# First stage by blocks of 128 channels, with later weight loads and table; delta rule with both halves transposed in a row

## The chip, the core and the metric

One core of a Trainium2 chip runs the whole program. Its engines work side by side and are tied by semaphores: TensorE (PE; PEld is its weight load), VectorE (DVE), ScalarE (ACT), GpSimd (POOL) and SyncE (SP), which here only issues DMA transfers. The metric is the device time of one execution in microseconds (us). Everything is float32. One `matmul` of the program appears in the trace as two MATMUL records.

## The reference

Two transformer blocks follow each other on a sequence of 1024 tokens of width 1024. The first block has two layers (neighbourhood attention, then grouped-query attention), the second one layer, whose mixer joins latent attention, a gated delta rule and a pooling mixer. Every layer ends in a mixture of experts. Two places matter here. The start of every layer scales and shifts the tokens by numbers made from a conditioning vector `c`:

```
c_act = silu(c)
mod = c_act @ ada_w[l] + ada_b[l]
h = x * (1.0 + scale) + shift
qkv = h @ w_qkv
```

The delta rule works in chunks of 64 tokens: for each chunk and head it forms the products of keys with keys and of queries with keys, multiplies them by decays, solves a unit lower triangular system, and carries a state from chunk to chunk:

```
a_mat = where(strict, (kb @ k.T) * decay, 0)
sol = triangular_solve(a_mat + eye, [v * beta, kb * exp(gc)])
qk = where(incl, (q @ k.T) * decay, 0)
v_new = u_i - w_i @ state
o_i = q_i @ state + qk_i @ v_new
state = state * gl_i + k_i.T @ v_new
```

## The kernel before

The program is a chain of stages with a barrier of all engines between them. Within a stage every engine has its own instruction stream, written by hand, in the order in which the code issues it; what one engine needs of another is a semaphore wait.

**The stage `front`** (lines 271 to 509) computes the scale and shift of the first layer, moves the tokens by them, and multiplies them with the 1024 x 3072 weight `na_w_qkv`. SP loads, in this order: four pieces of 2 MB with the 2048 columns of `ada_w` that hold shift and scale (L344), the tokens' first half (2 MB, L346, `hT`), the first 512 columns of `na_w_qkv` (2 MB, L340, `wt`), and the tokens' second half (2 MB, L348). PE multiplies each piece with the activated `c` (`partial`, L389: output rows of 32 in four column groups of the array, 512 columns each), ACT copies the sums, PE turns them into columns (`columns`, L396), DVE adds the bias and moves the eight channel blocks of the tokens' first half (L479). Only then can the projection begin. It consists of 48 items of eight matmuls each, 128 x 512 (`item`, L419 and L423), in four PSUM banks: item n may start once item n-4 has been evacuated, by DVE where n is even (L504, L449) and by ACT where it is odd (L463, L453).

Beside the projection the same stage computes all other modulation rows. For that SP streams 64 steps of 1 MB (L331) through a ring of four buffers, and DVE multiplies each with its activated `c` and adds it up (`weigh`, L489 and L492), two steps after each item. After item 4q+1, PE adds up quarter q over the partitions (`add_up`, L405). The bias rows for this are loaded by a DMA that repeats each row 32 times (`brow`, L335), at the first step of a quarter. The weights of the third, fourth and fifth block of columns are loaded before steps 18, 34 and 50, the last after the final step. GpSimd clears, fills and spreads the table of position biases for the next stage (L367 to L373, 25 DMAs) as soon as item 0 is done, and stores the finished rows after that.

**The stage `gdn`** (the delta rule, from line 2424 on) handles the eight token tiles in two halves f of four tiles. For each half, DVE normalises queries and keys (L2590) and makes three scaled copies (L2592, L2594, L2597) and two more (L2602, L2603); PE transposes keys, queries and scaled keys (`turn(f)`, L2849), ACT copies the six banks to SBUF (L2728 to L2730), PE multiplies them (`scores(f)`, L2863), and DVE multiplies the products by the decays (`decayed(f)`, L2610 and L2611). Both halves use PSUM banks 0 to 5 for the transposes and 0 to 3 for the products, so `turn(1)` waits until DVE has read `scores(0)`. Then DVE masks the matrices for level 0 of the solution (`level_input`, L2615), writes the decay of the last row of each chunk (`last_decay`, L2571, needed only after the solution), and goes through six levels of the triangular solution (L2636 to L2644), in which PE (L2874) and DVE alternate. ACT applies Silu to the gate `z` (L2747), and GpSimd multiplies it by the gain (L2816) as soon as that is done. In the last part of the stage ACT copies the pooling mixer's means (L2787) and squares the outputs (L2776).

## Time and profile before

| | us |
|---|---|
| Median of three runs | 3713.72 |
| Range of these runs | 3711.33 to 3714.51 |
| The profiled execution, its own time | 3712.36 |
| The profiled execution, its span | 3710.5 |
| PE busy in it | 3417.3 (92%) |
| DVE busy | 1618.9 (44%) |

The span runs from the first to the last instruction; 1.9 us of the execution's own time lie around it. PE is busy for 92% of the span, so the places where PE waits, or runs at the lower clock, are where time can be found. The stage `front` takes from 0 to about 372 us, and PE computes without a break from 34.3 us on. The stage `gdn` takes from 3010 to 3186 us; PE is busy there for a good part of the time, but waits in many short gaps.

### The profile page before, as it was taken

The numbers are of one execution on the slowest core, as the hardware profiler recorded it, in microseconds if no ns is written. First come the engines' busy times: TensorE is split into PE (matmuls) and PEld (weight loads), VectorE is DVE, ScalarE is ACT, GpSimd is POOL, SyncE is SP. The second block draws the span as 40 slices with busy tenths as digits, with TensorE's granted clock in tenths as the row PEclk, the third lists the DMA queues.
The fourth block names the chain that finished last, engine by engine and source line by source line (L and its number), as shares of the span: only waits on it lengthen the run. The fifth ranks groups of instructions, "written<-read, shape, count | busy, mean of one in ns | idle before, by whom it ended". The sixth has DMA issues, their size and how long they took to land. (4 is left out here: it accounts for less than half of the span.)

```text
span 3710.5 us, 51510 instructions
## 1 busy us (share of the span) xinstructions
PE 3417.3 (92%) x20876; PEld 1742.5 (47%) x20876; DVE 1618.9 (44%) x2553; ACT 815.8 (22%) x1815; POOL 364.4 (10%) x355
## 2 busy tenths in 40 slices
PE   7999999899999899999997999998899978998996
PEld 3444565433333344777754333333555658553332
DVE  3760886510111475777756111113332865462114
ACT  0000660100000122555501000000333551111112
POOL 1000300210000000000001200000000920003110
PEclk9999999999999999999998999999999989999998
DMA  9980211599999621000023999997323301319996
GB/s 383 360 318 0 92 67 71 223 409 426 424 423 422 243 91 52 31 1 1 1 92 160 390 426 425 427 421 305 118 81 108 123 1 61 119 65 361 419 418 265
DMA packets 146837, 818.41 MB, mean 221 GB/s; under 512 B 30019, under 2 KB 35779, under 8 KB 100518
## 3 DMA queue, kind: packets, MB, share of 16 engines
q1 hardware_dynamic: 117622, 737.20, 49.9%
q0 software_dynamic: 25808, 68.88, 4.8%
q10 hardware_dynamic: 3168, 8.96, 0.6%
q8 instruction: 172, 2.82, 0.3%
q14 instruction: 67, 0.55, 0.0%
HBM read 752.52 MB, written 82.55 MB: 225 GB/s over the span
## 5 line engine op out<-in xcount | busy, mean ns | idle before, releaser
L2289 PE MATMUL m_yp<-m_w,m_hidT 128*32 128x512 f32 (+2 forms) x2248 | 381.2, 600 | 12.0 <-issue 6.1
L2266 PE MATMUL m_up<-m_w,m_xT 128*32 128x512 f32 (+2 forms) x1792 | 304.2, 605 | 25.9 <-DMA m_w<-in_moe_w_up 25.9
L2266 PE MATMUL m_gp<-m_w,m_xT 128*32 128x512 f32 (+2 forms) x1792 | 297.4, 594 | 8.4 <-DVE m_xT L1910 4.5
L2047 DVE TENSOR_TENSOR m_hid<-m_sg,m_up 128x512 f32<-128x512 f32 x42 | 28.9, 687 | 572.9 <-PE m_up L2266 572.9
L2042 DVE TENSOR_TENSOR m_yt<-m_yp,keep_flat 128x512 f32<-128x512 f32 x128 | 82.4, 685 | 403.8 <-PE m_yp L2289 394.6
L419 PE MATMUL front_acc<-front_hT,front_wt 128*128 128x512 f32 x512 | 224.5, 599 | 5.8 <-DMA front_wt<-in_na_w_qkv 5.8
L2289 PEld LDWEIGHTS m_yp<-m_w,m_hidT 128*32 128x32 f32 (+2 forms) x2248 | 123.0, 124 | 222.7 <-issue 217.7
L2266 PEld LDWEIGHTS m_up<-m_w,m_xT 128*32 128x32 f32 (+2 forms) x1792 | 104.8, 126 | 219.8 <-issue 219.8
L2347 ACT ACTIVATE m_sg<-m_gp 128x512 f32<-128x512 f32 (+1 forms) x64 | 33.5, 524 | 768.7 <-PE m_gp L2266 549.6
L1202 PE MATMUL n_acc<-n_wt,n_hT 128*128 128x512 f32 (+2 forms) x512 | 192.2, 532 | 2.8 <-DMA n_wt<-in_w_in 2.1
L2266 PEld LDWEIGHTS m_gp<-m_w,m_xT 128*32 128x32 f32 (+2 forms) x1792 | 97.4, 123 | 202.3 <-issue 197.1
L253 ACT ACTIVATE gqa_probs<-gqa_scores,gqa_top 128x1024 f32<-128x1024 f32 x128 | 142.5, 1113 | 161.2 <-DVE gqa_top L222 161.2
L912 PE MATMUL n_acc<-n_wt,n_hT 128*128 128x512 f32 x384 | 170.0, 603 | 0.9 <-DMA n_wt<-in_gqa_w_qkv 0.9
L222 DVE TENSOR_REDUCE gqa_top<-gqa_scores 128x1 f32<-128x1024 f32 x128 | 150.7, 1219 | 42.1 <-PE gqa_scores L174 42.1
L2258 PE MATMUL m_gp<-m_w,m_xT 128*32 128x512 f32 (+2 forms) x912 | 155.9, 594 | 6.0 <-DMA m_w<-in_moe_w_up 3.5
L492 DVE SCALAR_TENSOR_TENSOR keep_flat<-v,front_cact,keep_flat 128x2048 f32<-128x2048 f32 x56 | 131.6, 2350 | 65.5 <-DMA v<-in_ada_w 44.6
L419 PEld LDWEIGHTS front_acc<-front_hT,front_wt 128*128 128x128 f32 x512 | 97.7, 192 | 132.0 <-issue 131.3
L1202 PEld LDWEIGHTS n_acc<-n_wt,n_hT 128*128 128x128 f32 x512 | 98.0, 194 | 85.9 <-issue 78.1
L164 PE MATMUL gqa_turn<-keep_ident,gqa_probs 128*128 128x128 f32 x1024 | 137.0, 277 | 0.2 <-ACT gqa_probsT L249 0.2
L164 PEld LDWEIGHTS gqa_turn<-keep_ident,gqa_probs 128*128 128x128 f32 x1024 | 113.6, 142 | 48.9 <-issue 48.9
L174 PE MATMUL gqa_scores<-k1T,q1T 64*128 64x512 f32 x512 | 130.6, 624 | 4.5 <-ACT gqa_probs L253 2.5
L193 PE MATMUL gqa_out<-gqa_probsT,v 128*64 128x128 f32 x2048 | 125.9, 276 | 0.8 <-ACT gqa_probsT L249 0.8
(502 smaller groups left out, 4984.2 us busy)
## 6 DMA issues: line engine op xcount, KB each, us to landing
m_w<-in_moe_w_gate SPq DMA_DIRECT2D x64, 2048.0 KB, 28.7
m_w<-in_moe_w_up SPq DMA_DIRECT2D x64, 2048.0 KB, 27.8
m_w<-in_moe_w_down SPq DMA_DIRECT2D x64, 2048.0 KB, 29.8
v<-in_ada_w SPq DMA_DIRECT2D x40, 1024.0 KB, 12.6
m_w<-in_moe_w_gate SPq DMA_DIRECT2D x32, 1024.0 KB, 28.2
m_w<-in_moe_w_up SPq DMA_DIRECT2D x32, 1024.0 KB, 29.6
m_w<-in_moe_w_down SPq DMA_DIRECT2D x32, 1024.0 KB, 31.0
v<-in_w_mod SPq DMA_DIRECT2D x24, 1024.0 KB, 11.0
```

What stands on the lines that cost most here:

```text
L164: last = pe.transpose(turn[f % TURN][:, i * P:(i + 1) * P], src, ident[:, :])
L174: last = pe.matmul(scores[h][:, c * 512:(c + 1) * 512], qT[half, j, t * P:(t + 1) * P], kT[half, 2 * j // SHARE, c * 512:(c + 1) * 512], s ...
L193: pe.matmul(out[h * HEAD:(h + 1) * HEAD, 0:P], v[:, k, kv * HEAD:(kv + 1) * HEAD], probsT[:, n % 2, h, k], start=k == 0, stop=k == TILES - 1)
L222: dve.tensor_reduce(top[:, n % 2, h:h + 1], scores[h][:, :], AX.X, ALU.max, negate=True).then_inc(max_ready, 1)
L253: act.activation(probs[:, n % 2, h], scores[h][:, :], ACT.Exp, bias=top[:, n % 2, h:h + 1], accum_out=total[:, n % 2, h:h + 1]).then_inc(p ...
L419: last = pe.matmul(acc[n % 4][:, :], wt[:, c % 2, k, i * P:(i + 1) * P], hT[:, k, half * 512:(half + 1) * 512], start=k == 0, stop=k == KC ...
L492: dve.scalar_tensor_tensor(total[:, q % 2], mw[:, s % RING], by, total[:, q % 2], ALU.mult, ALU.add).then_inc(weighed, 1)
L912: last = pe.matmul(acc[t % 2][:, c], hT[:, t % 2, k], wt[:, k, c * 512:(c + 1) * 512], start=k == 0, stop=k == KC - 1)
L1202: last = pe.matmul(acc[c][:, 0:n1 - n0], hT[:, t % 2, k], wt[:, k, n0:n1], start=k == 0, stop=k == KC - 1)
L2258: last = pe.matmul(gp[j][part, :].rearrange("p (m f) -> p m f", m=2), xT[:, j, k, part], w[:, home:home + 2, k * F:(k + 1) * F], start=k = ...
L2266: last = pe.matmul(acc[part, 0:F], xT[:, j, k, part], w[:, place_of[m_, r][0], k * F:(k + 1) * F], start=k == 0, stop=k == KC - 1)
L2289: last = pe.matmul(yp[e][part, :], hidT[:, k, part], w[:, place_of["d", r][0], k * D + e * 512:k * D + (e + 1) * 512], start=k == 0, stop= ...
```

## The change

**In `front`** the first 34 us are cut into channel blocks. The host lays the first 2048 columns of `ada_w` out anew (`first_mod`): piece k holds, for all inputs, the shift and scale of the 128 channels of block k. SP loads one small table (`first_cols`), then for each of the eight k the piece of the modulation (1 MB), the tokens' block (256 KB) and the weights' block (256 KB), then the tokens' second half as before. PE computes block k's partial sums (eight matmuls of 256 columns, two in a row for each of the four column groups), turns them into two columns, and DVE moves the block. As soon as block k is there, PE adds its contribution to the first four items (`by_channels`), two matmuls before the next `partial` and two behind it. Three matmuls on a tile of ones are put ahead. DVE does the first two `weigh` steps inside its loop over k. Items 4 to 47 stay as they were, but `add_up` of the first three quarters comes after items 7, 10 and 13 instead of 5, 9 and 13; the weights are loaded before steps 26, 42 and 58; the bias rows with the fourth step of a quarter; and GpSimd first stores six rows and only then builds the table.

**In `gdn`** DVE normalises both halves first, PE transposes both halves and then multiplies both, with separate PSUM banks for the halves; the transposed banks are handed to ACT one by one; `last_decay` is split and stands after levels 1 and 2; GpSimd multiplies the gate only when `uw_done[0]` is there, after the solution; and ACT squares the first outputs before it copies the pooling means.

The diff, cut to its core, first `front`:

```diff
-    KC, CW, QW, FIRST, RING = D // P, 512, 2048, 4, 4
+    KC, CW, QW, RING, BANKS, LEAD = D // P, 512, 2048, 4, 4, 2
...
-                    if k == 0:
+                    if k == 3:
...
-                first = quarter_of(0)[0]
-                for m in range(FIRST):
-                    sp.dma_start(first_buffer(m), first[:, 2 * m:2 * m + 2, :]).then_inc(first_in[m], 16)
-                sp.dma_start(sel[:, :], a["mod_sel"]).then_inc(s_in, 16)
-                sp.dma_start(hT[:, :, 0:512], xT[:, :, 0:512]).then_inc(x_in[0], 16)
-                load_weights(0)
-                sp.dma_start(hT[:, :, 512:S], xT[:, :, 512:S]).then_inc(x_in[1], 16)
+                sp.dma_start(first_cols[:, :], a["first_cols"]).then_inc(c_in, 16)
+                for k in range(KC):
+                    sp.dma_start(first_buffer(k), a["first_mod"][:, k]).then_inc(m_in[k], 16)
+                    sp.dma_start(hT[:, k, 0:512], xT[:, k, 0:512]).then_inc(x_in[k], 16)
+                    sp.dma_start(wt[:, 0, k], wv[:, k, 0:CW]).then_inc(w0_in[k], 16)
+                sp.dma_start(hT[:, :, 512:S], xT[:, :, 512:S]).then_inc(x1_in, 16)
                 for s in range(RING):
                     load_step(s)
                 load_weights(1)
                 for s in range(RING, STEPS):
-                    if s in (18, 34, 50):
-                        load_weights(2 + (18, 34, 50).index(s))
+                    if s in (26, 42, 58):
+                        load_weights(2 + (26, 42, 58).index(s))
                     load_step(s)
                 load_weights(5)
...
-                pool.wait_ge(mm_done, 1)
+                def store_row(q):
+                    pool.wait_ge(row_added, q)
+                    pool.dma_start(quarter_of(q)[3], row[0:P:32, q % 2]).then_inc(stored[q % 2], 16)
+
+                for q in range(1, 7):
+                    store_row(q)
                 pool.dma_start(flat_table, zero[:, :]).then_inc(cleared, 16)
...
-                for q in range(1, QUARTERS):
-                    dst = quarter_of(q)[3]
-                    pool.wait_ge(row_added, q)
-                    pool.dma_start(dst, row[0:P:32, q % 2]).then_inc(stored[q % 2], 16)
+                for q in range(7, QUARTERS):
+                    store_row(q)
...
-                def partial(m):
-                    pe.wait_ge(first_in[m], 16)
-                    for n in range(2):
-                        k = 2 * m + n
-                        for g in range(4):
-                            last = pe.matmul(mp[32 * g:32 * g + 32, :], cact[:, 0, k:k + 1].to_broadcast([P, 32]),
-                                             first_buffer(m)[:, n, g * CW:(g + 1) * CW], start=k == 0, stop=k == KC - 1)
+                def partial(k):
+                    pe.wait_ge(m_in[k], 16)
+                    if k >= 2:
+                        pe.wait_ge(part_cp, k - 1)
+                    for c in range(KC):
+                        g = c // 2
+                        last = pe.matmul(mps[k % 2][32 * g:32 * g + 32, 0:2 * P], cact[:, 0, c:c + 1].to_broadcast([P, 32]),
+                                         first_buffer(k)[:, c], start=c % 2 == 0, stop=c % 2 == 1)
                     last.then_inc(part_done, 1)
 
-                def columns():
-                    pe.wait_ge(part_cp, 1)
-                    for i in range(4):
-                        last = pe.matmul(ms[:, 4 * i:4 * i + 4], part[:, i * P:(i + 1) * P], sel[:, :], start=True, stop=True)
+                def columns(k):
+                    pe.wait_ge(part_cp, k + 1)
+                    if k >= 2:
+                        pe.wait_ge(cols_done, k - 1)
+                    for i in range(2):
+                        last = pe.matmul(ms[k % 2][:, i:i + 1], part[:, k % 2, i * P:(i + 1) * P], sel, start=True, stop=True)
                     last.then_inc(sum_done, 1)
...
+                def by_channels(k, items):
...
+                    pe.wait_ge(w0_in[k], 16)
+                    pe.wait_ge(h_ready, k + 1)
+                    for n in items:
+                        last = pe.matmul(acc[n][:, :], wt[:, 0, k, n * P:(n + 1) * P], hT[:, k, 0:512], start=k == 0, stop=k == KC - 1)
+                        if k == KC - 1:
+                            last.then_inc(mm_done, 1)
...
+                pe.wait_ge(ones_set, 1)
+                for _ in range(3):
+                    pe.matmul(acc[0][0:32, :].rearrange("p (m n) -> p m n", n=32), ones[:, :], ones[:, :].unsqueeze(1).to_broadcast([P, 16, 32]),
+                              start=True, stop=True)
                 pe.wait_ge(act_done, 1)
...
+                partial(0)
+                columns(0)
+                partial(1)
+                columns(1)
+                for k in range(KC):
+                    by_channels(k, range(0, 2))
+                    if k + 2 < KC:
+                        partial(k + 2)
+                    by_channels(k, range(2, BANKS))
+                    if k + 2 < KC:
+                        columns(k + 2)
+                after = {max(4 * q + 1, 3 * q + 4): q for q in range(1, QUARTERS)}
+                for n in range(BANKS, ITEMS):
                     item(n)
-                    if n % 4 == 1 and n > 4:
-                        q = n // 4
-                        if q < QUARTERS:
-                            add_up(q)
+                    if n in after:
+                        add_up(after[n])
...
+                def move(k, half):
+                    part_of = hT[:, k, half * 512:(half + 1) * 512]
+                    dve.tensor_scalar(part_of, part_of, col[:, 2 * k + 1:2 * k + 2], col[:, 2 * k:2 * k + 1], ALU.mult, ALU.add).then_inc(h_ready, 1)
+
...
+                for k in range(KC):
+                    pair = slice(2 * k, 2 * k + 2)
+                    dve.wait_ge(sum_done, k + 1)
+                    dve.tensor_tensor(col[:, pair], ms[k % 2][:, 0:2], bcol[:, pair], ALU.add).then_inc(cols_done, 1)
+                    dve.wait_ge(x_in[k], 16)
+                    dve.wait_ge(cols_done, k + 1)
+                    move(k, 0)
+                    if k >= KC - LEAD:
+                        weigh(k - KC + LEAD)
+                dve.wait_ge(x1_in, 16)
+                for k in range(KC):
+                    move(k, 1)
+
...
-                    for s in (2 * n, 2 * n + 1):
+                    for s in (2 * n + LEAD, 2 * n + 1 + LEAD):
...
+        TURN_BANK = {"k": ((0, 3), (6, 7)), "q": ((2, 5), (0, 3)), "kb": ((1, 4), (2, 1))}
+        KQ_BANK = (4, 0)
```

then `gdn` and the host:

```diff
-                scale_keys(0)
+                norm_keys(0)
+                norm_keys(1)
+                scale_values(0)
                 scale_rest(0)
-                scale_keys(1)
+                scale_values(1)
                 decayed(0)
                 scale_rest(1)
...
-                last_decay()
...
+                    if 1 <= lv <= 2:
+                        last_decay(lv - 1)
...
                     for m in range(2):
...
+                out_squares(0)
                 act.wait_ge(pool_in, 16 * 5)
                 copy_means(0)
-                out_squares(0)
...
                 pool.wait_ge(z_ready, 1)
+                pool.wait_ge(uw_done[0], 1)
...
+                    pe.wait_ge(normed, f + 1)
                     if f:
-                        pe.wait_ge(qk_ready, 1)
+                        pe.wait_ge(dec_ready, 4)
...
+                    for kind, src in (("k", qkv[:, :, W:2 * W]), ("q", qkv[:, :, 0:W]), ("kb", kb[:, :, :])):
+                        if kind == "q" and f == 0:
                             pe.wait_ge(dec_ready, 2)
-                        if b == 1:
+                        if kind == "kb":
                             pe.wait_ge(kb_ready, f + 1)
                         for m in range(2):
+                            if f and kind != "k":
+                                pe.wait_ge(turns_copied, {"q": 1, "kb": 3}[kind] + (2 * m if kind == "kb" else m))
                             for i in range(4):
                                 t, g = HALF * f + 2 * m + i // 2, i % 2
-                                last = pe.transpose(ps[:, 3 * m + b, i * P:(i + 1) * P], src[:, t, g * P:(g + 1) * P], ident[:, :])
-                    last.then_inc(turned, 1)
+                                last = pe.transpose(ps[:, TURN_BANK[kind][f][m], i * P:(i + 1) * P], src[:, t, g * P:(g + 1) * P], ident[:, :])
+                            last.then_inc(turned, 1)
...
-                    pe.wait_ge(turns_copied, 6 * (f + 1))
+                    pe.wait_ge(turns_copied, 12 if f else 8)
...
                 turn(0)
+                turn(1)
                 scores(0)
-                turn(1)
                 scores(1)
...
+    first_bias = inputs["ada_b"][0, 0:2 * D].reshape(2, D // P, P).transpose(2, 1, 0).reshape(P, 2 * D // P)
+    every_32nd = (np.arange(P)[:, None] % 32 == 0).astype(np.float32)
+    inputs["first_cols"] = np.concatenate([inputs["c"][0].reshape(P, D // P), inputs["c_2"][0].reshape(P, D // P), first_bias, every_32nd], axis=1)
+    inputs["first_mod"] = inputs["ada_w"][0, :, 0:2 * D].reshape(P, D // P, 2, D // P, P).transpose(0, 3, 1, 2, 4).reshape(P, D // P, D // P, 2 * P)
```

What stands in a row on the engines, at three places. First PE at the start of `front`, before:

```order
L389 MATMUL front_mp<-q0T,front_cact 32x512 x16
L389 MATMUL front_mp<-k0T,front_cact 32x512 x16
L396 MATMUL front_ms<-front_sel,front_part 128x4 x4
L419 MATMUL front_acc<-front_hT,front_wt 128x512 x48
L405 MATMUL front_mp<-keep_flat,front_ones 32x512 x4
```

and now (the pattern of the four rows before the last repeats for every block):

```order
L443 MATMUL front_acc<-front_ones 32x512 x3
L394 MATMUL front_mp<-q0T,front_cact 32x256 x8
L403 MATMUL front_ms<-front_first_cols,front_part 128x1 x2
L394 MATMUL front_mp<-q0T,front_cact 32x256 x8
L403 MATMUL front_ms<-front_first_cols,front_part 128x1 x2
L411 MATMUL front_acc<-front_hT,front_wt 128x512 x2
L394 MATMUL front_mp<-q0T,front_cact 32x256 x8
L411 MATMUL front_acc<-front_hT,front_wt 128x512 x2
L403 MATMUL front_ms<-front_first_cols,front_part 128x1 x2
L411 MATMUL front_acc<-front_hT,front_wt 128x512 x2
```

The 32 matmuls of items 0 to 3, which stood in one row behind all partial sums, are now spread between them.

Second DVE between the first modulation and item 0's evacuation in `front` (`front_hT` is moved in place; `keep_flat<-v` is a `weigh` step; `q0T<-front_acc` is the evacuation of item 0), before:

```order
L469 TENSOR_TENSOR front_col<-front_ms,front_bcol 128x16
L472 TENSOR_SCALAR front_col<-front_col 128x4x2
L479 TENSOR_SCALAR front_hT<-front_hT,front_col 128x512 x16
L504 TENSOR_SCALAR q0T<-front_acc 128x512
L489 TENSOR_SCALAR keep_flat<-v,front_cact 128x2048
```

and now, from block 6 on:

```order
L516 TENSOR_TENSOR front_col<-front_ms,front_first_cols 128x2
L506 TENSOR_SCALAR front_hT<-front_hT,front_col 128x512
L499 TENSOR_SCALAR keep_flat<-v,front_cact 128x2048
L516 TENSOR_TENSOR front_col<-front_ms,front_first_cols 128x2
L506 TENSOR_SCALAR front_hT<-front_hT,front_col 128x512
L502 SCALAR_TENSOR_TENSOR keep_flat<-v,front_cact,keep_flat 128x2048
L506 TENSOR_SCALAR front_hT<-front_hT,front_col 128x512 x8
L535 TENSOR_SCALAR q0T<-front_acc 128x512
```

Two `weigh` steps and the eight moves of the second half now stand ahead of the evacuation of item 0.

Third DVE in `gdn`, from the normalisation to level 0, before:

```order
L2590 TENSOR_TENSOR k<-k,keep_raw 128x4x512
L2592 TENSOR_TENSOR gdn_kb<-k,gdn_beta 128x1024
L2594 TENSOR_TENSOR keep_flat<-k,gdn_beta 128x16x64
L2597 TENSOR_TENSOR keep_flat<-k,gdn_nbe 128x16x64
L2610 TENSOR_TENSOR k<-gdn_ps,gdn_dec 128x1024
L2611 TENSOR_TENSOR gdn_KQ<-gdn_ps,gdn_dec 128x16x64
L2602 TENSOR_TENSOR gdn_qd<-k,gdn_eg 128x1024
L2603 TENSOR_TENSOR gdn_KQ<-k,gdn_kdf 128x16x64
L2610 TENSOR_TENSOR k<-gdn_ps,gdn_dec 128x1024
L2611 TENSOR_TENSOR gdn_KQ<-gdn_ps,gdn_dec 128x16x64
L2615 TENSOR_TENSOR gdn_keys<-k,keep_flat 128x1024 x2
L2571 TENSOR_TENSOR gdn_keys<-keep_flat,gdn_glx 64x8x64 x8
```

(these begin with the second half's normalisation), and now, from the normalisation of both halves:

```order
L2621 TENSOR_TENSOR k<-k,keep_raw 128x4x512
L2623 TENSOR_TENSOR gdn_kb<-k,gdn_beta 128x1024
L2621 TENSOR_TENSOR k<-k,keep_raw 128x4x512
L2623 TENSOR_TENSOR gdn_kb<-k,gdn_beta 128x1024
L2628 TENSOR_TENSOR keep_flat<-k,gdn_beta 128x16x64
L2595 SCALAR_TENSOR_TENSOR gdn_nbe<-gdn_eg,gdn_beta 128x32
L2631 TENSOR_TENSOR keep_flat<-k,gdn_nbe 128x16x64
L2636 TENSOR_TENSOR gdn_qd<-k,gdn_eg 128x1024
L2637 TENSOR_TENSOR gdn_KQ<-k,gdn_kdf 128x16x64
L2628 TENSOR_TENSOR keep_flat<-k,gdn_beta 128x16x64
L2631 TENSOR_TENSOR keep_flat<-k,gdn_nbe 128x16x64
L2644 TENSOR_TENSOR k<-gdn_ps,gdn_dec 128x1024
```

The second normalisation has moved ahead of the scaled copies, and the eight rows of L2571 stand no longer ahead of the levels.

## Rows read from the trace of the kernel before

**Rows 1.** Stretches: busy us (count) per engine from PE to POOL, PEclk, DMA share, GB/s

```profile
0.00:34.30 34.30, 12.64 (x72) 3.08 (x73) 4.08 (x10) 2.10 (x3) 0.97 (x6) 0.83 0.97 377
...
3010.00:3068.10 58.10, 35.85 (x334) 27.04 (x336) 41.15 (x50) 29.61 (x49) 4.51 (x1) 0.71 0.00 1
```

**Rows 2.** Timeline, PE in `front`: start, busy us, line, count, [idle before <-releaser]

```profile
8.84 3.64 PE L389 MATMUL front_mp<-q0T,front_cact 128*32 128x512 f32 x16 [8.84 <-ACT front_cact L458]
13.40 1.92 PE L389 MATMUL front_mp<-q0T,front_cact 128*32 128x512 f32 x16 [0.91 <-DMA q0T<-in_ada_w]
...
27.44 1.03 PE L396 MATMUL front_ms<-front_sel,front_part 128*128 128x4 f32 x8 [0.82 <-ACT front_part L453]
34.30 8.09 PE L419 MATMUL front_acc<-front_hT,front_wt 128*128 128x512 f32 x12 [5.84 <-DMA front_wt<-in_na_w_qkv]
...
59.83 10.46 PE L419 MATMUL front_acc<-front_hT,front_wt 128*128 128x512 f32 x24
```

**Rows 3.** Stretches of `front`, columns as in rows 1

```profile
18.30:23.00 4.70, 2.80 (x16) 0.47 (x16) 0.00 (x0) 0.00 (x0) 0.00 (x0) 0.60 1.00 406
34.30:39.50 5.20, 5.20 (x6) 2.16 (x7) 0.00 (x0) 0.00 (x0) 0.00 (x0) 0.50 1.06 397
...
41.10:47.00 5.90, 5.90 (x16) 2.55 (x15) 5.53 (x10) 0.00 (x0) 0.67 (x1) 1.00 1.02 274
```

**Rows 4.** Timeline, DVE in `front`, columns as in rows 2

```profile
28.99 3.74 DVE L479 TENSOR_SCALAR front_hT<-front_hT,front_col 128x512 f32<-128x512 f32 x8
41.13 1.00 DVE L479 TENSOR_SCALAR front_hT<-front_hT,front_col 128x512 f32<-128x512 f32 x2 [8.39 <-DMA front_hT<-in_x_turned]
...
44.78 0.68 DVE L504 TENSOR_SCALAR q0T<-front_acc 128x512 f32<-128x512 f32 x1
...
49.33 2.35 DVE L492 SCALAR_TENSOR_TENSOR keep_flat<-v,front_cact,keep_flat 128x2048 f32<-128x2048 f32 x1 [2.67 <-DMA v<-in_ada_w]
```

**Rows 5.** Timeline, PE in `gdn` where two kinds of 64*64 matmuls meet

```profile
3138.23 0.33 PE L2918 MATMUL gdn_ps<-gdn_KQ,gdn_early 64*64 64x128 f32 x2
3138.26 0.38 PE L2906 MATMUL gdn_ps<-keep_flat,k 64*64 64x128 f32 x3
```

**Rows 6.** Costliest groups of 2621.4 to 2623.2: 16 matmuls into one column group

```profile
L1219 PE MATMUL n_up<-n_latT,n_ukv 128*64 128x128 f32 x16 | 2.0, 276 | 0.0
```

**Rows 7.** Timeline, DVE in `gdn`

```profile
3028.08 2.29 DVE L2590 TENSOR_TENSOR k<-k,keep_raw 128x2048 f32<-128x2048 f32 x1 [0.35 <-ACT keep_raw L2721]
...
3042.05 1.22 DVE L2610 TENSOR_TENSOR k<-gdn_ps,gdn_dec 128x1024 f32<-128x1024 f32 x1
3043.18 1.21 DVE L2611 TENSOR_TENSOR gdn_KQ<-gdn_ps,gdn_dec 128x1024 f32<-128x1024 f32 x1
...
3056.13 1.23 DVE L2610 TENSOR_TENSOR k<-gdn_ps,gdn_dec 128x1024 f32<-128x1024 f32 x1 [9.48 <-PEq L2867]
...
3062.86 5.24 DVE L2571 TENSOR_TENSOR gdn_keys<-keep_flat,gdn_glx 64x512 f32<-64x512 f32 x8
...
3069.28 1.21 DVE L2638 TENSOR_TENSOR k<-keep_flat,gdn_ps 128x1024 f32<-128x1024 f32 x1
...
3092.22 1.22 DVE L2642 TENSOR_TENSOR k<-k,gdn_ps 128x1024 f32<-128x1024 f32 x1 [4.05 <-PE gdn_ps L2874]
```

**Rows 8.** Stretch of `turn(1)` in `gdn`, columns as in rows 1

```profile
3044.45:3049.83 5.38, 5.38 (x24) 4.97 (x24) 2.21 (x2) 0.00 (x0) 0.00 (x0) 0.50 0.00 0
```

**Rows 9.** Timeline, PE in `gdn`

```profile
3052.96 3.03 PE L2863 MATMUL gdn_ps<-gdn_keys 64*64 64x128 f32 x64 [3.13 <-ACT gdn_keys L2730]
3061.95 6.39 PE L2874 MATMUL gdn_ps<-keep_flat,gdn_keys 64*64 64x64 f32 x128 [5.96 <-DVE gdn_keys L2615]
3071.68 6.62 PE L2874 MATMUL gdn_ps<-k,gdn_keys 64*64 64x64 f32 x128 [3.34 <-DVE gdn_keys L2615]
```

**Rows 10.** One line, L2615 of DVE, 3056 to 3070: min/median/max ns, starts

```profile
L2615 DVE TENSOR_TENSOR gdn_keys<-k,keep_flat x2: 1211/2303/3395, 3058.4 to 3061.7; 128x1024 f32<-128x1024 f32 x2
```

**Rows 11.** Timeline, POOL in `gdn`

```profile
3056.21 4.51 POOL L2816 TENSOR_TENSOR gdn_z<-gdn_z,keep_flat 128x2048 f32<-128x2048 f32 x1 [71.38 <-ACT gdn_z L2747]
```

128 lines of the change are left out of this document (55 added, 73 removed).

## The prediction

> **What bounds the kernel now.** I read the stretches first [rows 1]. In the first 34.3 us the DMA engines are busy for 97% at 377 GB/s while PE works for 12.64 us: the DMA bounds. The timeline of PE [rows 2] shows the waits (8.84, 0.91, 0.82, 5.84 us), and that item 0 begins when `na_w_qkv` is there, at 34.30. From then on PE computes without a break, so a start earlier by x ends the stage earlier by x, as long as nothing else becomes late. In `gdn`, PE is busy in 35.85 of the 58.1 us before the levels, at a mean clock of 0.71, so there I read DVE [rows 7]: it computes nearly all the time, except for 9.48 us before 3056.13, in which `turn(1)`, six ACT copies and `scores(1)` follow each other. In the levels PE leads, and DVE waits 4.05 us for it (before 3092.22).
>
> **Front: the DMA side.** 12 MB must land, in the same order of size as before. The tokens' second half, the last of them, makes DVE start at 41.13 [rows 4]; w0, the one before it, was there at 34.30 [rows 2]. At 377 to 406 GB/s [rows 1, 3], 2 MB take 5.2 to 5.6 us, so the second half should land at about 34.2 + 5.4 = 39.6, one DMA issue earlier than its wait on record would say; 41.1 is the late bound. The blocks come every 1.5 MB, 1,572,864 bytes by 0.377 to 0.406 MB/us: 3.9 to 4.2 us (I take 3.9, since the stretch from 18.3 to 23.0 without the beginning ran at 406). All eight blocks are there by 34.2.
>
> **Front: the PE side.** Per block PE has four matmuls of 512 columns, a `partial` and two `columns`. 24 records take 10.46 us at full clock [rows 2], 0.436 each with the odd `add_up`; I use 0.429 and two records to a matmul: 4 x 0.857 = 3.43. The old `partial` is 16 records of 512 in 1.92 us at full clock and 3.64 at half [rows 2]; the new one has 16 records of 256: 0.88 to 0.96. `columns` had 8 records in 1.03 us, at the half clock to judge by its time; four now: 0.26 to 0.52, I take 0.45 with its start. Two changes of the array's shape cost about 0.2 (an estimate: what is left of 1.92 above 16 x 0.429 / 4 = 1.72). Sum 3.43 + 0.88 + 0.45 + 0.2 = 4.95 us, more than the 3.9 of the DMA, so **PE sets the pace**. The second modulation block is there at about 9.6, with its `partial` and `columns` the loop begins at 11.6 to 12.9 and ends after six full rounds and two short ones: 11.6 + 6 x 4.95 + 2 x 3.43 = 48.2; up to 50.8 if part of it runs at half clock. ACT's copies and DVE's first moves (0.47 each, 3.74 for eight [rows 4]) lie beside it.
>
> **Front: what item 4 waits for.** Item 4 needs the moved second half and item 0's evacuation. DVE's stream now has the two `weigh` steps ahead of both. Step 0 and step 1 are the next 2 MB behind the second half: 39.6 + 2.5 = 42.1 and 44.6; the second costs 2.35 [rows 4] and ends at 47.0. Then eight moves, 3.74: 50.7; evacuation 0.68 [rows 4]: **item 4 starts at 51.8** with 0.4 for semaphores. Before, it stood behind item 3 at 34.30 + 32 matmuls: six records took 5.20 us at the half clock [rows 3], the other 58 take 24.9: 64.4. Gain 12.6. But PE then sits idle for 51.8 - 48.2 = 3.6 us. Before 18.3 it idled 3 us and the next stretch ran at 0.60, and after 5.84 us idle at 0.50 for 5.20 us [rows 3], where six records cost 2.6 more than at full clock. I charge 2.2: **net gain of the front 10.4**. With no clock loss and the loop from 11.6 it would be 12.6; with the late bounds, under the rivals, 5.1.
>
> **Front: what costs nothing.** `add_up` and the bias row's DMA are only moved in time; the stretch with that DMA ran at 274 GB/s [rows 3], and it now falls behind the start of item 4. The weights are loaded eight steps later than before, some 27 us by the pace of the items (3.43 us a step), and are wanted about 56 us after the old place: I keep nothing for it. GpSimd stores rows first and builds the table later; both end long before the stage does. The squares ahead of the means in `gdn` alter only ACT's order before a wait for a DMA. The three matmuls on ones run before the first block is there.
>
> **Delta rule.** From the first normalisation (3028.08, 2.29 [rows 7]) DVE now has a second one, then 14 operations like those at 3042.05 and 3043.18, 1.13 apart, and a small one of 0.2, up to the end of `decayed(1)`: 3028.08 + 2 x 2.31 + 14 x 1.14 + 0.2 = 3048.9, with one more semaphore 3049.2, in place of 3056.13 + 1.23 + 1.13 = 3058.49. **Gain 9.3**, if DVE waits for nobody. It wants `scores(0)` at 3042.0. PE can begin the last transposes at 3035.0 (both scaled keys), and one `turn` took 5.38 us at half clock [rows 8], one `scores` 3.03 [rows 9]: in the worst case 3034 + 5.4 + 3.5 = 3042.9, 0.9 late; at full clock 1.5 early. Next, `level_input`: beside GpSimd's z operation one of the two took 3.395 us where the other took 1.211 [rows 10, 11], and PE's level 0 began only behind it (3061.95). The z operation is now behind the solution: **2.18** more. The eight operations of `last_decay` (5.24 [rows 7]) leave this place and come back, four at a time (2.62), behind levels 1 and 2, where DVE has 4.05 us per level to spare: hidden; if not, they cost 5.24. So PE begins level 0 at 3049.2 + 1.21 + 0.1 = 3050.5 and, at 6.39 for both halves [rows 9], finishes the first at about 3053.8; then DVE's subtraction runs that stood at 3069.28 [rows 7]. **Gain 15.4.** PE's own product now bounds, not DVE, so of 9.3 + 2.2 + 5.2 = 16.7 some 1.3 are lost. Level 1 took 6.62 us after a gap of 3.34 [rows 9], longer than level 0; without the gap I give 0.4: **15.8 in all**, between 12.5 (DVE 0.9 late, z operation hurting at its new place by its 2.18) and 16.9.
>
> GpSimd's z operation in its new place meets DVE's copies from PSUM. L2610 (3056.13) read PSUM beside it and took 1.23 against 1.22 without it [rows 7, 11], so nothing is charged. The Trainium skill ("SBUF — State Buffer", section "SBUF: two separate sides") says that the port pair which both engines share is an exclusive lock, held for a whole instruction, when DVE has two SBUF inputs: the long L2615 agrees, and by it copies from PSUM go free too.
>
> **Sum**: 10.4 + 15.8 = 26.2. The profiled execution took 3712.36; 3712.36 - 26.2 = 3686.2. It lies 1.36 below the median of 3713.72, so the predicted median is **3687.5**.
>
> **Rivals.**
> A: matmuls of one column group in a row block those behind them. The new `partial` issues two per group in a row. 16 records of 128 columns into one group took 2.0 us [rows 6], 0.125 each, so 256 columns cost 0.43 a matmul, and with each group's second overlapping the next group's first the `partial` takes 5 x 0.43 = 2.1 instead of 0.9: round 6.2, start 12.9, item 4 at 57.0 to 59.4 (first blocks at half clock), net gain 7.5 to 5.1. Against it: at 3138.23 two matmuls of L2918 started before three of L2906 that stand ahead of them in the program [rows 5], so one that waits for its tile does not hold the next. Time with 5.1: 3713.7 - 5.1 - 15.8 = **3692.8**. The Trainium skill ("TensorE: Matmul & The Clock Gate", section "The mechanism") calls MATMULs "strict FIFO, no reordering"; rows 5 speak against it. Chance 0.08.
> B: DMA late. If steps 0 and 1 land as late as before, when DVE began step 1's successor at 49.33 [rows 4], item 4 starts at 49.33 + 2.35 + 3.74 + 0.68 + 0.1 = 56.2 and the clock loss is whole (2.6): gain 5.6, **3692.3**. Chance 0.08.
> C: `last_decay` is not hidden in the levels: 15.8 - 5.24 = 10.6, **3692.7**. Chance 0.08.
> D: the modulation stream bounds the front. Items ask for a step per 3.43 us; at 274 GB/s, seen beside the repeating DMA [rows 3], a step of 1,048,576 bytes takes 3.83. Over 62 steps, 3.86 us each (272 GB/s) would eat the whole gain; at 4.0 us (262 GB/s) the loss is 35.3 and the time 3687.5 + 35.3 = **3722.8**. Against it: the step ran at 2.5 us outside that stretch, and the stretch is 6 us in a quarter of 27. Chance 0.02.
> E: the change does not do what it says, above all because PE's waits put the old order back (`scores` late, loop over k bound by DVE): half of the gain, 3700. Chance 0.03.
>
> **How the numbers follow.** The forecast has 0.71: gain 24.2 to 30, that is 3683.7 to 3689.5 by the PE bounds of the front (12.6) and of `gdn` (16.9) above and a DVE late by 0.9 with a whole clock loss below. The range takes in A, B, C and two of them together with the low bound of `gdn`: **3680 to 3699**; outside lie D, E and three mishaps at once. This kernel's measurement can tell 0.2% (7.4 us) from no change: faster 0.95, within 0.03, slower 0.02.
>
> **What would show it.** In the front: item 4's start (51.8), PE's gap of 3 to 4 us ahead of it and a granted clock below 1 behind it; a `partial` of 0.9 against 2.1 us (A); the end of the second `weigh` step at 47.0 (B). In `gdn`: no long wait of DVE before the second half's products; 25.8 us from the first normalisation to the first half's subtraction of level 0, against 41.2; both L2615 at 1.21; a DVE gap left in levels 1 and 2 (C). A clock that stays low in the loop over the blocks, where PE stops at every block, would make the front wrong by several us.

## Result and the profile of the changed kernel

| | before | changed |
|---|---|---|
| Median, us (four runs each) | 3712.99 | 3688.0 |
| Range, us | 3711.33 to 3714.51 | 3681.5 to 3693.09 |
| The profiled execution, its own time | 3712.36 | 3681.5 |
| Stage `front`: time of its last barrier | 377.39 | 367.40 |
| Item 4 starts at | 64.55 | 54.43 |
| Stage `gdn`, barrier to barrier | 175.53 | 160.29 |

The ratio is 0.9933 (95% interval 0.9921 to 0.9945): 25.0 us faster, where 26.2 were forecast. In the profiled executions the front is 10.0 us and the delta rule 15.2 us shorter. These executions differ by 30.9; the 5.6 that are left lie in stages that the change doesn't touch. The largest piece is the stage behind the first mixture of experts, which took 228.8 us from barrier to barrier before and 225.3 after. In the twelve kernels of the experiments below, none of which touches it either, it took 226.1 to 228.5 us, so most or all of this piece is scatter and no gain.

The barrier of the front stands at 377.39 us before (and not at about 372, as said above).

PE at the start of the front of the changed kernel (start, busy us, line, count, idle before):

```profile
6.18 1.09 PE L394 MATMUL front_mp<-q0T,front_cact 128*32 128x256 f32 x16 [0.27 <-DMA q0T<-in_first_mod]
...
10.28 1.96 PE L394 MATMUL front_mp<-q0T,front_cact 128*32 128x256 f32 x16 [1.90 <-DMA q0T<-in_first_mod]
...
13.64 3.76 PE L411 MATMUL front_acc<-front_hT,front_wt 128*128 128x512 f32 x4
17.34 1.93 PE L394 MATMUL front_mp<-q0T,front_cact 128*32 128x256 f32 x16
...
46.87 7.11 PE L411 MATMUL front_acc<-front_hT,front_wt 128*128 128x512 f32 x16
54.43 27.73 PE L434 MATMUL front_acc<-front_hT,front_wt 128*128 128x512 f32 x64 [0.45 <-DVE q0T L535]
```

Projection work starts at 13.64 in place of 34.30 [rows 2]. The first `partial` takes 1.09 us. The second, behind a pause of 1.90 us, takes 1.96, at half the clock. The granted clock of the stretches says the same (columns: PE, PEld, DVE, ACT, POOL busy, PEclk, DMA share, GB/s):

```profile
8.40:10.20 1.80, 0.00 (x0) 0.00 (x0) 0.70 (x2) 0.00 (x0) 0.00 (x0) 0.63 0.95 357
...
13.60:19.20 5.60, 5.60 (x22) 1.86 (x22) 0.70 (x2) 0.00 (x0) 0.00 (x0) 0.51 1.04 419
19.20:24.30 5.10, 5.10 (x33) 2.36 (x29) 0.70 (x2) 0.38 (x1) 0.00 (x0) 1.00 1.03 411
```

The clock is not lost at the same moment in every execution. The trace of the changed kernel has it at half from 8.9 to 19.1 us. The same front in another execution (the run of the front alone, below) has it at half from 11.0 to 17.8, by its record of the stretch that reads 0.51 above:

```profile
13.60:19.20 5.60, 5.60 (x23) 2.12 (x23) 0.70 (x2) 0.39 (x1) 0.00 (x0) 0.62 1.04 418
```

There item 4 starts at 53.73, 0.7 us earlier than here. This is how far one and the same front differs from execution to execution at item 4.

DVE on the way to item 4:

```profile
44.27 1.29 DVE L499 TENSOR_SCALAR keep_flat<-v,front_cact 128x2048 f32<-128x2048 f32 x1 [1.51 <-DMA v<-in_ada_w]
47.05 0.16 DVE L516 TENSOR_TENSOR front_col<-front_ms,front_first_cols 128x2 f32<-128x2 f32 x1 [1.49 <-PE front_ms L403]
...
47.78 2.35 DVE L502 SCALAR_TENSOR_TENSOR keep_flat<-v,front_cact,keep_flat 128x2048 f32<-128x2048 f32 x1
50.04 3.73 DVE L506 TENSOR_SCALAR front_hT<-front_hT,front_col 128x512 f32<-128x512 f32 x8
53.69 0.69 DVE L535 TENSOR_SCALAR q0T<-front_acc 128x512 f32<-128x512 f32 x1
```

The first `weigh` step (44.27) waits for its data, which landed at 44.25. The data of the second landed at 46.74, but the step begins at 47.78: it stands behind the move of block 7, and that waits for PE's `columns(7)` (the 1.49 at 47.05). So DVE's chain is late by the DMA first and by PE's pace on top, and PE and DVE reach item 4 within 0.45 us of each other.

In the delta rule, DVE has no wait before the decayed products, where it had 9.48 us [rows 7]:

```profile
3014.13 2.29 DVE L2621 TENSOR_TENSOR k<-k,keep_raw 128x2048 f32<-128x2048 f32 x1 [0.34 <-ACT keep_raw L2757]
...
3028.10 1.22 DVE L2644 TENSOR_TENSOR k<-gdn_ps,gdn_dec 128x1024 f32<-128x1024 f32 x1
...
3033.77 1.22 DVE L2645 TENSOR_TENSOR gdn_KQ<-gdn_ps,gdn_dec 128x1024 f32<-128x1024 f32 x1
3034.90 2.35 DVE L2649 TENSOR_TENSOR gdn_keys<-k,keep_flat 128x1024 f32<-128x1024 f32 x2
...
3039.98 1.22 DVE L2673 TENSOR_TENSOR k<-keep_flat,gdn_ps 128x1024 f32<-128x1024 f32 x1 [1.59 <-PE gdn_ps L2915]
...
3057.66 2.60 DVE L2603 TENSOR_TENSOR gdn_keys<-keep_flat,gdn_glx 64x512 f32<-64x512 f32 x4
3061.80 1.22 DVE L2677 TENSOR_TENSOR k<-k,gdn_ps 128x1024 f32<-128x1024 f32 x1 [1.53 <-PE gdn_ps L2915]
```

The subtraction of level 0 (L2673) comes 25.85 us after the first normalisation; before it was 41.20 (3069.28 - 3028.08). Both L2649 take 2.35 together, so none is stretched as in [rows 10]. Behind level 1 DVE still waits for PE (1.53) after four `last_decay` operations (L2603), so these are hidden. PE's side, where `scores` of both halves end 1.3 us before DVE wants the first:

```profile
3019.94 1.97 PE L2890 MATMUL gdn_ps<-keep_ident,k 128*128 128x128 f32 x16
...
3022.71 1.98 PE L2904 MATMUL gdn_ps<-gdn_keys 64*64 64x128 f32 x64
3024.87 1.98 PE L2904 MATMUL gdn_ps<-gdn_keys 64*64 64x128 f32 x64 [0.18 <-PE gdn_ps L2904]
```

### The profile page after: what moved, and what is told of

The parts are those of the page before. It is cut to its first block and busy times, and to the rows that moved or that the text cites. A ratio compares the mean times of both kernels' runs of the same rounds, so it can differ in the third digit from the quotient of the medians.

```text
span 3679.7 us, 51768 instructions
## 1 busy us (share of the span) xinstructions
PE 3420.4 (93%) x20970; PEld 1738.1 (47%) x20970; DVE 1617.9 (44%) x2560; ACT 818.3 (22%) x1822; POOL 364.8 (10%) x355
## 5 line engine op out<-in xcount | busy, mean ns | idle before, releaser
L434 PE MATMUL front_acc<-front_hT,front_wt 128*128 128x512 f32 x448 | 194.4, 594 | 0.4 <-DVE q0T L535 0.4
L434 PEld LDWEIGHTS front_acc<-front_hT,front_wt 128*128 128x128 f32 x448 | 84.5, 190 | 110.5 <-issue 107.9
## 6 DMA issues: line engine op xcount, KB each, us to landing
m_w<-in_moe_w_down SPq DMA_DIRECT2D x32, 1024.0 KB, 30.2
```

What stands on the lines that cost most here:

```text
L434: last = pe.matmul(acc[n % BANKS][:, :], wt[:, c % 2, k, i * P:(i + 1) * P], hT[:, k, half * 512:(half + 1) * 512], start=k == 0, stop=k = ...
```

## The experiments

The times of one kernel scatter by some us from execution to execution (3681.5 to 3693.1 for the changed one), so a single edit is read in its stage: in the front by item 4's start and the stage's last barrier, in the delta rule by the time X from the first normalisation to the first half's subtraction of level 0. The executions with one and the same code say what a difference in these must exceed. The old front has its barrier at 377.39 and 377.70, the new one at 367.40 and 367.85. Four executions with the same loop have item 4 at 53.73, 53.76, 54.43 and 54.55. X is 25.84 or 25.85 in five executions of the new delta rule. Where a kernel has two edits, they lie in these two stages, with barriers between them.

### Each half of the change alone

Edit: the function `front` (with its host arrays) of the changed kernel beside `gdn` of before, and the other way round.

> The new front stage with the delta rule of before. Theory (the two parts add, and nothing else of the program gains): the barrier behind the front comes 10.0 us earlier, as in the changed kernel, with item 4 at 54.4; the delta rule keeps its 175.8 us; time 3713.0 - 10.0 = 3703.0. Rival (something between the two stages gains or loses with them): the two parts alone don't add up to the 25.0 us of the whole, by more than the 3 us or so that the runs scatter.

> The new delta rule behind the front stage of before. Theory: the stage takes 160.5 us in place of 175.8, the front ends at 377.4, time 3713.0 - 15.2 = 3697.8. Rival as for the other half.

Measured: front alone 3710.81 beside 3717.48 us of before in the same session (ratio 0.9982, interval 0.9972 to 0.9992), barrier at 367.85, 9.5 us earlier; delta rule alone 3703.03 (0.9965, interval 0.9952 to 0.9977), stage 160.06 us, X 25.85. The two ratios multiply to 0.9947 beside 0.9933 for the whole; each interval is 0.1% wide to either side, so the parts add as far as these runs can tell. The front alone missed its expected 3703.0: its time fell by 6.7 us and not by 10, but the interval of that reaches from 3.0 to 10.4, and the barrier's 9.5 lies in it. The old delta rule took 174.36 us beside the new front, with X at 40.04 in place of 41.20. Its `turn(1)` took 4.2 us there and 5.38 before, part of it at the full clock. So the gain up to X is 14.2 us by the one execution of the old stage and 15.4 by the other.

### No weigh step in the loop; last_decay put back

```diff
-    KC, CW, QW, RING, BANKS, LEAD = D // P, 512, 2048, 4, 4, 2
+    KC, CW, QW, RING, BANKS, LEAD = D // P, 512, 2048, 4, 4, 0
...
                     level_input(0, f)
+                for c in range(2):
+                    last_decay(c)
                 for lv in range(LEVELS):
...
-                    if 1 <= lv <= 2:
-                        last_decay(lv - 1)
```

> Two edits in two stages, each read in its own stage. Front: no weigh step ahead of the second half's moves (LEAD 0). The prediction's step (DVE's chain sets item 4) would bring item 4 from 54.4 to 52.0. The trace of the changed kernel has PE's loop over the blocks end at 53.98 and says: item 4 at 54.0, 0.4 us gained. Delta rule: the eight last_decay operations are put back ahead of the levels. Theory: PE's product leaves DVE 1.6 us there, so of their 5.2 us 3.6 are lost: the first half's subtraction of level 0 (X) comes 29.4 us after the first normalisation instead of 25.85, and the stage takes 164.1. Rivals: 5.2 lost (165.7), or given back in the levels, where the behind operations would be missing (160.5).

Item 4 starts at 52.98, where 54.0 was expected, but this loop also ran 0.8 us earlier (46.03 in place of 46.87 for its last part), as it does in two executions with an unchanged loop. There is no pause between the loop and item 4: the loop's end is the bound, and DVE's chain was worth some 0.6 us:

```profile
46.03 7.11 PE L411 MATMUL front_acc<-front_hT,front_wt 128*128 128x512 f32 x16
52.98 3.60 PE L434 MATMUL front_acc<-front_hT,front_wt 128*128 128x512 f32 x8
```

The barrier came at 365.85, 1.5 us earlier. X came at 29.45, 3.60 us later, as the first theory had it to 0.05:

```profile
3039.61 5.25 DVE L2603 TENSOR_TENSOR gdn_keys<-keep_flat,gdn_glx 64x512 f32<-64x512 f32 x8
3044.88 1.22 DVE L2673 TENSOR_TENSOR k<-keep_flat,gdn_keys 128x1024 f32<-128x1024 f32 x1
```

The wait of 1.59 us for PE's product is used up, the rest of 5.25 is lost, and the last level came 3.8 us later too, so nothing was given back. The stage took 162.74, less than 164.1, because what follows (from the last operation of the last level to the barrier) scatters from 54.7 to 58.4 us over the executions of this study.

### Two filling matmuls; GpSimd's z operation early

```diff
                 partial(0)
                 columns(0)
+                for _ in range(2):
+                    pe.matmul(acc[0][0:32, :].rearrange("p (m n) -> p m n", n=32), ones[:, :], ones[:, :].unsqueeze(1).to_broadcast([P, 16, 32]),
+                              start=True, stop=True)
                 partial(1)
...
                 pool.wait_ge(z_ready, 1)
-                pool.wait_ge(uw_done[0], 1)
```

> Two edits in two stages. Front: two more matmuls on ones between the columns of block 0 and the partial sums of block 1, where PE idles 1.9 us. Theory: the clock stays full, the partial of block 1 takes 1.1 instead of 2.0 us, the loop over the blocks ends near 50.2 instead of 54.0; but item 4 then waits for DVE's two weigh steps and eight moves, and starts at 53.6. Rival 1: the clock falls all the same, item 4 at 54.4. Rival 2: DVE doesn't bound, item 4 at 50.7. Delta rule: GpSimd's z operation no longer waits for the solution. Theory (it holds up only DVE operations with two SBUF inputs): it starts 13.5 us after the first normalisation, runs 4.5 us, the decayed operations beside it keep 1.22, and the next operation with two SBUF inputs (L2636) is held up by 1.7, the subtraction of level 0 comes 27.5 us after the normalisation instead of 25.85. Rival (every DVE operation is held up): 4 us or more lost. Rival (nothing but L2615 is): no loss.

The clock stayed full (the second row below: 1.09 us in place of 1.96), the loop's last part began 3.6 us earlier (43.26), and then PE waited 2.81 us for DVE; item 4 at 53.18. It waited 1.19 us more ahead of item 6 and 0.5 at the fourth `add_up`, and the barrier came at 368.16: 0.8 us **later** than in the changed kernel. Alone, this edit of the front gains nothing at the stage's end:

```profile
8.41 1.90 PE L449 MATMUL front_acc<-front_ones 128*32 128x512 f32 x4
10.59 1.09 PE L394 MATMUL front_mp<-q0T,front_cact 128*32 128x256 f32 x16 [0.27 <-DMA q0T<-in_first_mod]
...
43.26 7.11 PE L411 MATMUL front_acc<-front_hT,front_wt 128*128 128x512 f32 x16
53.18 14.00 PE L434 MATMUL front_acc<-front_hT,front_wt 128*128 128x512 f32 x32 [2.81 <-DVE q0T L538]
68.37 14.00 PE L434 MATMUL front_acc<-front_hT,front_wt 128*128 128x512 f32 x32 [1.19 <-DVE q0T L538]
```

Here DVE's second `weigh` step waits for its data itself and not for PE:

```profile
46.52 2.35 DVE L505 SCALAR_TENSOR_TENSOR keep_flat<-v,front_cact,keep_flat 128x2048 f32<-128x2048 f32 x1 [0.47 <-DMA v<-in_ada_w]
```

In the delta rule, DVE and then GpSimd:

```profile
3034.90 1.22 DVE L2647 TENSOR_TENSOR k<-gdn_ps,gdn_dec 128x1024 f32<-128x1024 f32 x1
3036.03 1.22 DVE L2648 TENSOR_TENSOR gdn_KQ<-gdn_ps,gdn_dec 128x1024 f32<-128x1024 f32 x1
3037.16 3.27 DVE L2639 TENSOR_TENSOR gdn_qd<-k,gdn_eg 128x1024 f32<-128x1024 f32 x1
```

```profile
3034.44 4.91 POOL L2857 TENSOR_TENSOR gdn_z<-gdn_z,keep_flat 128x2048 f32<-128x2048 f32 x1 [55.41 <-ACT gdn_z L2788]
```

Beside GpSimd the two operations that read PSUM keep 1.22 us, and the next, with two SBUF inputs, takes 3.27: GpSimd ends at 3039.35, this one 1.1 us behind that. 2.05 us are lost, X comes at 27.90, 0.4 later than expected. The charge is that of the prediction (2.18) to 0.13, and it fell on the first operation of that kind.

### Both front edits together; the old order of the scaled copies

```diff
                 norm_keys(0)
-                norm_keys(1)
                 scale_values(0)
                 scale_rest(0)
+                norm_keys(1)
                 scale_values(1)
```

> Two edits in two stages. Front: the two filling matmuls and LEAD 0 together. Theory: with the clock kept and DVE freed, item 4 starts at 50.7, 3.7 us earlier than in the changed kernel, more than the sum of the two edits alone (0.4 and 0.8), since each alone leaves the other's bound standing. Rival: another bound (DMA, w blocks) keeps it at 52 or later. Delta rule: DVE again makes the first half's scaled copies before it normalises the second half; PE's new order and the new banks stay. Theory: PE then idles 4.8 us between the two turns, falls to the half clock, and scores(0) ends 5.0 us later than DVE wants it (1.0 if the clock stays full): the subtraction of level 0 comes 27 to 31 us after the normalisation, 31 being what I expect. Rival: DVE's order carries all of the gain of 9.3 and PE's order and banks carry none: 35 us.

Item 4 started at 50.07 with no pause before it: 4.4 us earlier than in the changed kernel. Each edit alone left the other's bound standing. But the barrier came at 366.44, only 1.0 us earlier. The time was given back at three `add_up` (3.3 us of waits), which the table below takes up.

X came at 29.34, where 31 was expected. PE and DVE:

```profile
3032.94 3.68 PE L2893 MATMUL gdn_ps<-keep_ident,k 128*128 128x128 f32 x16 [5.20 <-DVE k L2624]
3036.41 1.27 PE L2893 MATMUL gdn_ps<-keep_ident,gdn_kb 128*128 128x128 f32 x8
3037.61 1.98 PE L2907 MATMUL gdn_ps<-gdn_keys 64*64 64x128 f32 x64
```

```profile
3039.81 1.23 DVE L2647 TENSOR_TENSOR k<-gdn_ps,gdn_dec 128x1024 f32<-128x1024 f32 x1 [3.40 <-PEq L2911]
```

The clock was at half behind 5.20 us of idling, as expected, but it was back at full at 3036.9, before the scaled keys were done, so 3.5 us were lost, not 5. The rival (DVE's order alone carries 9.3) falls: with the new banks and PE's new order the old order of copies costs 3.5.

### Weights, bias rows and table where they were; banks handed over all at once

```diff
-                    if s in (26, 42, 58):
+                    if s in (18, 34, 50):
...
-                    if k == 3:
+                    if k == 0:
...
-                for q in range(1, 7):
-                    store_row(q)
+                pool.wait_ge(mm_done, 1)
                 pool.dma_start(flat_table, zero[:, :])
...
-                        act.wait_ge(turned, 6 * f + i + 1)
+                        act.wait_ge(turned, 6 * f + 6)
```

> Two edits in two stages. Front: the later weights (18, 34, 50), the bias rows with the first step of a quarter, and GpSimd's table ahead of the stores, as before the change. Theory: the repeating DMA takes about 1.9 us of transfer ahead of weigh step 0, step 1 lands later, item 4 starts 0.9 us later (55.3), the rest costs nothing, and the front is 0.9 us longer. Rival: the table's or the weights' transfers hold up the modulation stream and PE waits elsewhere in the stage: several us more. Delta rule: ACT copies the six transposed banks only when all six are there. Theory: scores(0) comes some 1.5 us later, which is what it was early: the stage keeps 160.5 us within 0.3. Rival: handing over singly is worth 1.5 us or more.

The theory on the front (0.9 us longer) was wrong by much. The rival, that PE waits elsewhere in the stage, was right in kind, and more than its "several us": the barrier came at 380.63, 13.2 us later than in the changed kernel and 3.2 later than **before** the change. The profiled time was 3708.21. Item 4 at 57.11, then:

```profile
57.11 30.79 PE L433 MATMUL front_acc<-front_hT,front_wt 128*128 128x512 f32 x64 [3.62 <-DVE q0T L534]
...
136.20 1.94 PE L420 MATMUL front_mp<-keep_flat,front_ones 128*32 128x512 f32 x8 [4.50 <-DVE keep_flat L501]
138.07 29.57 PE L433 MATMUL front_acc<-front_hT,front_wt 128*128 128x512 f32 x64
```

PE waits at the third `add_up` for the eighth `weigh` step of its quarter. Each of the two waits is followed by work at a lower clock (64 records in 30.79 and 29.57 us, 27.73 elsewhere). Handing over singly was worth nothing: X 25.85.

### The three put back one by one

> The changed kernel, with GpSimd's table built right behind item 0 again. The run with three things put back at once made the front 13.2 us longer than the changed kernel's: 2.7 at item 4, 3.1 in the stretch behind it at a lower clock, 0.2, and 7.2 around the third add_up, where PE waited 4.5 us for the modulation stream and came back at the half clock. Theory: the table's 25 transfers take their time from the DMA engines at 50 to 75 us, before the first add_up, which has 9.4 us to spare: PE waits nowhere more, front within 0.5 of 367.4. Rival: the transfers move the whole stream by 2.9 us or more (the spare time at the third add_up), and PE waits there.

> The changed kernel, with the later weights loaded before steps 18, 34 and 50 again. Theory: 2 MB, some 5.4 us of transfer, now go ahead of step 18, so the steps of the third quarter come 5.4 us later, with 2.9 us to spare before: PE waits about 2.5 us at the third add_up (at 125.7), loses 1 to 3 us more where it comes back at the lower clock, and the front ends at 371 to 373. Rival (the wait came from the bias row or the table): no wait at the third add_up, 367.4.

> The changed kernel, with the bias row's repeating DMA in the first step of each quarter again, so ahead of or beside weigh step 0. Theory: it delays steps 0 and 1 by the time it takes, item 4 comes at 57.1, PE idles 3.6 us before it and computes at a lower clock behind it: 2.7 + 3.1 = 5.8 us, front at 373.2; no wait at the third add_up. Rival (the stream's delay stays until then): a wait of up to 2 us there as well, 375 to 376.

The edits are the three parts of the diff above. What each kernel's front did; "spare" is the time from the end of a quarter's last `weigh` step to the `add_up` that needs it (0.1 means that PE waited), and the last column is free of how early the loop began. The second row is the changed front once more, in the run of the front alone:

| | item 4 | spare at third, fourth `add_up` | barrier | from item 4 to it |
|---|---|---|---|---|
| before | 64.55 | 0.7, 4.9 | 377.39 | 312.8 |
| changed | 54.43 | 2.9, 1.8 | 367.40 | 313.0 |
| changed, again | 53.73 | 2.0, 0.6 | 367.85 | 314.1 |
| table back | 54.55 | 0.1, 0.1 | 372.76 | 318.2 |
| weights back | 53.76 | 0.1, 4.2 | 370.73 | 317.0 |
| bias rows back | 56.71 | 6.5, 5.5 | 371.38 | 314.7 |
| all three back | 57.11 | 0.1, 7.0 | 380.63 | 323.5 |
| no weigh step in the loop | 52.98 | 1.9, 0.8 | 365.85 | 312.9 |
| filling matmuls | 53.18 | 1.0, 0.1 | 368.16 | 315.0 |
| both front edits | 50.07 | 0.1, 0.1 | 366.44 | 316.4 |

**Bias rows**: as expected in kind. The repeating DMA delays `weigh` steps 0 and 1, on which item 4 waits, and PE idles (first row below); 4.0 us in all, where 5.8 were expected, with less loss of clock. **Weights**: as expected, a wait of 2.99 us at the third `add_up` (second row), 3.3 us by the barrier. **Table**: the rival was right. The 25 transfers of GpSimd are not small together: one of 372 KB, eight of 22.5 and sixteen of 192, 3.6 MB in all, as much as three and a half `weigh` steps. They push the whole stream: 5.4 us, most of it in waits at two `add_up` and at an evacuation (1.85) that stands behind late `weigh` steps on DVE (last two rows). A wait of 0.73 at an earlier evacuation isn't the table's, since the unchanged front of the run of the front alone has it too, at 68.45. Alone the three cost 12.7, together 13.2. Each is one execution, and the same front differs by 0.45 between two.

```profile
56.71 29.43 PE L434 MATMUL front_acc<-front_hT,front_wt 128*128 128x512 f32 x64 [2.66 <-DVE q0T L535]
```

```profile
129.01 1.07 PE L421 MATMUL front_mp<-keep_flat,front_ones 128*32 128x512 f32 x8 [2.99 <-DVE keep_flat L502]
```

```profile
100.05 7.13 PE L433 MATMUL front_acc<-front_hT,front_wt 128*128 128x512 f32 x16 [1.85 <-DVE q0T L534]
...
129.97 1.07 PE L420 MATMUL front_mp<-keep_flat,front_ones 128*32 128x512 f32 x8 [0.99 <-DVE keep_flat L501]
```

### No matmuls on ones ahead; the rest copies behind level 0's masks

```diff
-                for _ in range(3):
-                    pe.matmul(acc[0][0:32, :].rearrange("p (m n) -> p m n", n=32), ones[:, :], ones[:, :].unsqueeze(1).to_broadcast([P, 16, 32]),
-                              start=True, stop=True)
...
                 decayed(0)
-                scale_rest(1)
                 decayed(1)
...
                     level_input(0, f)
+                scale_rest(1)
+                dve.wait_ge(scaled, 8)
```

> Two edits in two stages. Front: the three matmuls on ones at the start are left out. Theory: only the partial of block 0 gets slower (2.0 instead of 1.1), block 1's DMA hides that, item 4 at 54.4 as before. Rival: the clock then rises one round later, which costs 2.4 us: item 4 at 56.8. Delta rule: the two rest copies of the second half are made behind the masks of level 0 (with one wait for them). Theory: DVE idles 1.6 us there now, so PE's product starts 2.3 us earlier and the subtraction 1.5 us earlier (24.4 us after the normalisation); the stage takes 159.0. Rival: PE is not ready earlier, no gain.

Item 4 at 54.83, 0.4 later than in the changed kernel and 0.3 to 1.1 later than in the four executions with the same loop: of the work ahead of the loop, block 0's `partial` and `columns` got slower (1.96 and 1.01 in place of 1.09 and 0.61). So the three matmuls at the start bring little as long as the clock falls behind them anyway. X at 24.30, 1.55 us earlier: the first normalisation began at 3018.50, and DVE no longer waits for PE's product:

```profile
3042.79 1.22 DVE L2671 TENSOR_TENSOR k<-keep_flat,gdn_ps 128x1024 f32<-128x1024 f32 x1
```

The last level comes 1.56 earlier too.

### Two versions that join what helped

The changed kernel with the filling matmuls, `LEAD` 0 and the later rest copies; then the same with every `add_up` from the third on one item later:

```diff
-                after = {max(4 * q + 1, 3 * q + 4): q for q in range(1, QUARTERS)}
+                after = {4 * q + 2 + (q == 1): q for q in range(1, QUARTERS)}
```

> The changed kernel with the filling matmuls, LEAD 0 and the later rest copies. Theory: item 4 at 50.7 (front 3.7 shorter), the delta rule 159.0 us (1.5 shorter): 5.2 us less than the changed kernel's 3688.0, 3682.8. Rival: one of the two is taken back by a later bound, 3684 to 3687.

> The version with the filling matmuls, no weigh step in the loop and the later rest copies, and every add_up from the second on one item later (behind items 7, 10, 14, 18, 22, 26 and 30). There PE waited 0.86, 0.97 and 0.82 us at three add_ups, for a modulation stream that the DMA engines feed. Theory: 6.9 us later all steps are there, the waits are gone, and the front is 2.7 us shorter than that version's 365.9: 363.2; time 2.7 under it, 3686 beside a kernel of before of 3715.7 (ratio 0.992). Rival: DVE, which must add the row behind each add_up, now waits for PE and the stream falls behind further, PE waits as much elsewhere: no gain.

The first: 3688.69 us beside 3715.73 of before in its session, ratio 0.9927 (interval 0.9913 to 0.9941). That is 27.0 us of gain, where 30.2 were expected; the time itself lies above both theories, because before was 2.7 us slower there than in the first comparison. Item 4 at 50.17 (50.7 expected), but the barrier at 365.90 in place of 363.7: the rival was right, a later bound took 2.8 us back (315.7 us from item 4 to the barrier), at three `add_up`, of which one:

```profile
122.25 1.07 PE L421 MATMUL front_mp<-keep_flat,front_ones 128*32 128x512 f32 x8 [0.86 <-DVE keep_flat L505]
```

The second: the barrier at 363.21, where 363.2 was expected, no wait left (5.9 and 4.5 us to spare at the third and fourth `add_up`):

```profile
128.36 1.06 PE L421 MATMUL front_mp<-keep_flat,front_ones 128*32 128x512 f32 x8
```

3683.88 us beside 3712.39, ratio 0.9920 (interval 0.9907 to 0.9934). The profiles show its front 4.2 us and X 1.55 us under the changed kernel's. The times of the two kernels overlap, and so do the intervals of their ratios, so the stages show that it beats the changed kernel, and the totals don't.

## Why the prediction was right, and where its steps were not

**The total** (3687.5 against 3688.0) is right to less than the kernel's own scatter. The two halves are right as well: 10.4 forecast and 10.0 measured, 15.8 and 15.2. Their steps are not equally so. In the front three terms were wrong and cancelled.

**Front, the DMA side.** The blocks landed 4.14 us apart on average, where the prediction took 3.9 out of its 3.9 to 4.2. By the landings in the trace, the last block's weights were there at 36.4 and not at 34.2, the tokens' second half at 41.8 and not at 39.6, past the late bound of 41.1, and the first two `weigh` steps at 44.25 and 46.74 and not at 42.1 and 44.6. Everything that hangs on the DMA came some 2.2 us late.

**Front, PE's pace.** A round takes 5.10 us, 4.95 were worked out. But the loop ended at 53.98, not at 48.2. It began at 13.64 in place of 11.6 (2.0), most of its first round ran at half clock, 7.74 us in place of 4.95 (2.8), and the other rounds and the tail brought 1.0. The step that failed is "the loop begins at 11.6 to 12.9". The prediction had allowed a part at half clock, up to an end at 50.8, and had named a clock that stays low as what would make the front wrong. In the trace the clock is lost around a pause of 1.90 us, and the filling matmuls, which kept it up, brought the loop's last part forward by 3.6 us.

**Front, DVE's chain.** The second step's data landed 2.1 us later than the 44.6 worked out, and the step began another 1.0 later, at 47.78, because it stood behind a move that waits for PE. The prediction has the first on the DMA and the second not at all. The chain reached item 4 at 54.4, not 51.8.

**Front, the clock loss of 2.2.** There was none, since PE idled 0.45 us and not 3.6. So the gain of item 4 was 10.1 in place of 12.6, all of it kept. The net is near the forecast because two terms missed in opposite directions: 2.5 too much gain and 2.2 too much loss. That is luck and no sizing.

**Front, "what costs nothing".** Right as a price of the change as it is: from item 4 to the barrier it takes 313.0 us, as before (312.8). Wrong as a reading. The three moved groups of transfers carry the whole gain of the front: put back, they cost 13.2 us. The prediction asked whether a moved transfer comes in time; the question was what each would hold up if it stayed, once PE came 10 us sooner while the DMA engines, busy all the time, did not. The number for this was in the trace of before: its third `add_up` had 0.7 us to spare. Rival D had the right mechanism with the wrong form: the stream needn't fall behind the items' pace over 62 steps, it need only be late at one `add_up`.

**Delta rule.** `decayed(1)` ended 20.9 us after the first normalisation (21.1 worked out), X came at 25.85 (25.8). The single prices stood the test: z operation 2.05 (2.18), `last_decay` 3.6 of 5.2 with PE's product behind it, and hidden in the levels. At its new place (3104.88, 4.54 us) the z operation meets four copies from PSUM in DVE that keep 0.69 us each, so that charging nothing there was right. Of the stage's 15.2, 15.35 come up to X, 1.1 more up to the last level (0.4 forecast), and 1.2 go in the part behind, which scatters by more than that. Against the other execution of the old stage the gain up to X is 14.2. The count of DVE's operations decides the new X, to 0.01 us in five executions; the old one hung on PE's clock.

**Rivals.** A falls: the first `partial` takes 1.09 us, half of 2.1, and its records start in fours, at 6.18, 6.19, 6.21 and 6.22, though two matmuls of one column group stand in a row. (The 16 in rows 6, from which A took its price, are records and so eight matmuls, not sixteen.) The rule of the Trainium skill ("TensorE: Matmul & The Clock Gate", section "The mechanism") that MATMULs keep strict order does not hold here for matmuls in different column groups. B holds by half: the first two steps' data were 2.1 us late, where B had the second step begin at 49.33, 4.7 late. C falls by the wait of 1.53 us that is left. D is taken up above. For the z operation, the Trainium skill ("SBUF — State Buffer", section "SBUF: two separate sides") has a DVE instruction with two SBUF inputs wait for the port pair that GpSimd holds for a whole instruction. The run that moved it agrees: the operations that read PSUM kept 1.22 us, the one with two SBUF inputs took 3.27.

**The inner bounds** don't quite follow from their terms: 12.6 and 16.9 make 29.5 and not 30, 10.0 and 14.9 make 24.9 and not 24.2, and 15.8 less 0.9 and 2.18 is 12.7 and not 12.5. Nothing measured lies between.

What stays open: when exactly the clock falls in the front, why the end of the delta rule scatters, and how the front's transfers would have to be ordered for the DMA to keep up the 3.9 us a block.

## What to carry to other kernels

When the engine that bounds a stage is made to start earlier, work out the spare time at every place where it meets a stream that won't come earlier; here all eight `add_up` of before had less to spare (0.7 to 9.6 us) than the 10 us gained. Moving the transfers kept the gain, as the runs that put them back show; what the `add_up` moved by the change itself are worth was not tested alone. Look for the second bound before removing the first: the filling matmuls and the freed DVE each brought 1.5 us or less at item 4, both together 4.4, and that came out at the end only with the meeting points moved one item. Compare a difference with what the same code does in two executions: 0.8 us at item 4, 0.45 at the barrier. In a chain on one in-order engine, count operations by their start-to-start time: this gave the place of an instruction some 25 us later to 0.1 us in three forecasts of five; it missed by 0.4 where GpSimd held an operation up, and by 1.7 where PE's clock decided.

## What the runs showed of the hardware

In all seven executions of a front with the three matmuls on ones and without the filling ones, PE paused for 1.5 to 2.1 us (1.90 in the changed kernel) behind 2.2 us of work at full clock, and the granted clock went to half at some time from 8.9 to 12.1 us, to come back between 17.8 and 19.3. In the four with filling matmuls it stayed full. After 5.20 us of idling PE came back at half clock, and the clock was full again 3.9 us later. In the changed kernel, records for different 32-column groups started within 0.05 us of each other although each group's second matmul stood ahead of the next group's first. A GpSimd operation held up the DVE operation with two SBUF inputs, by 2.05 us, and let two that read PSUM pass at 1.22. Transfers of 3.6 MB started by GpSimd, beside a stream that had the DMA engines busy at 0.97 to 1.05 (the profile's share), delayed it by enough to cost PE 5.4 us.
